# A hybrid decoder trunk on one core: the first quarter's gates by one 64-column matmul per token, GpSimd making all low weights of that stage, scatter from panel 11

## The chip, the cores and the metric

The kernel runs on one core of a Trainium2 chip. The metric is the device time of one execution in microseconds. Times of the kernel before are those of three runs; the profile is of one further execution of the same program.

## The reference

Two layers, each a token mixer (a gated short convolution in layer 0, latent attention in layer 1) and then a PEER mixer, which is the part that matters here. 256 tokens of 1024 channels; 8 heads; 128 keys per half; 16384 experts, of which each token and head takes 16:

```python
q = (xc @ w_q).reshape(C, PEER_HEADS, 2, PEER_HALF)
s = jnp.einsum("chpd,hpnd->chpn", q, subkeys).astype(jnp.float32)
top_s, top_i = lax.top_k(s, PEER_TOPK)
cand = top_s[:, :, 0, :, None] + top_s[:, :, 1, None, :]
best_s, best_pos = lax.top_k(cand.reshape(C, PEER_HEADS, PEER_TOPK * PEER_TOPK), PEER_TOPK)
ia = jnp.take_along_axis(top_i[:, :, 0], best_pos // PEER_TOPK, axis=-1)
ib = jnp.take_along_axis(top_i[:, :, 1], best_pos % PEER_TOPK, axis=-1)
expert = ia * PEER_KEYS + ib
g = jax.nn.softmax(best_s, axis=-1).astype(xc.dtype)
act = jax.nn.gelu(jnp.einsum("chkd,cd->chk", u_tab[expert], xc), approximate=False) * g
return jnp.einsum("chk,chkd->cd", act, v_tab[expert])
```

## The kernel before, in words

The PEER mixer is not gathered. The kernel multiplies all tokens with all experts: 128 panels of `peer_u` (one first key each, 128 experts by 1024 channels), then the gelu, then a weight that is zero for experts not chosen, then 128 panels of `peer_v`. Float32 products are made of two reduced parts (float32r): ScalarE makes the high part of a panel (`split_hi`, a cast of `raw` to `w_hi`), and GpSimd or VectorE the low part (`split_lo`, `raw` minus `w_hi` to `w_lo`). A panel has 4 slots for raw and high parts, 2 for low ones. The low part of panel j waits for its high part and until panel j-2 is multiplied; the loading of panel j+4 waits for the low part of panel j. On TensorE a panel is 16 matmuls with the high part (L588, L589) and 8 with the low part (L593), each 256 columns.

Per layer the PEER mixer goes through these stages:

- *search* ("sel"): 22 panels, 16 of them queries. VectorE takes the best 16 of each half and of their sums (`select`, L1404 to L1448).
- *ahead*: 26 panels of `peer_u` (j = 0 to 25). In the first half VectorE ends `select`: it decodes ranks into rows and columns and key numbers (L1470 to L1526, the *decode*). `dec_done` tells TensorE that tile t is decoded, and TensorE turns it (`turn`, 33 matmuls) in front of panel `TURN[t]` = 11 or 13. ScalarE copies what was turned (`turned`), and VectorE splits the gates (`gate_part`).
- from panel `SCATTER` = 13 on, the gates of the first quarter of the first keys are *scattered*: 16 groups of 16 tokens, spread over the 13 panels by `groups_after`. For a group VectorE makes one-hot matrices of the second key (`second_key_hots`, L1538) and of the first key times the gate's two parts (`first_key_hots`, L1542 and L1547 twice). TensorE then does two matmuls of 32 columns per token, which sum the parts in the bank (`scatter`, L655). The two banks take turns by group, and ScalarE copies a bank out (`copy_gates`, L1007).
- *mix*: three loops over 64 panels, alternately `peer_u` and `peer_v`, which also scatter the next quarters' gates, and *last*, 32 panels of `peer_v`. There a group is one matmul of 64 columns per token (`scatter_side`, L643), which leaves the two parts side by side over both banks; ScalarE copies the first part (`copy_first`, L1015) and VectorE adds the second (`add_gates`, L1557).

The order on each engine is written out by hand. Low parts: GpSimd makes all of the convolution, the attention and the search and the first `POOL_AHEAD` = 6 of the ahead stage (`select_panels`). VectorE makes the other 20 of the ahead stage: eight inside the decode (`next_lo`), the rest one after each panel's groups (`experts`), and all of mix and last. GpSimd's queue otherwise holds loads of the modulation's rows (L1301), one per wait on VectorE.

After the last group VectorE multiplies the first weights (`weigh`), ScalarE and VectorE split them, and TensorE takes them in the first `peer_v` panel; meanwhile it clears four banks (L703) and does the first wide panel of mix (L609, L614).

Of the kernel before, what the change touches and what calls it, by code (L numbers as in the profile page):

```python
# [56 lines left out]
POOL_AHEAD = 6  # L57
EXP_AFTER = 5
TURN = (11, 13)
SCATTER = 13  # L60
# [49 lines left out]
def program(nc, xT_in, c_in, pos_in, vec_in, con_in, ada_in, pan_in, key_in, iota_in, u_in, v_in, out):  # L110
    ctx = ExitStack()
    with ctx:
# [334 lines left out]
        def _(pe):  # L447
# [199 lines left out]
            def scatter(l, par, count):  # L647

                pe.wait_ge(hot_ready, count)
                pe.wait_ge(g_read, count)  # L650
                hb = hot_b[:, par, :].rearrange("p (t b) -> p t b", t=GT)
                hg = hot_g[:, par, :].rearrange("p (t x a) -> p t x a", x=2, t=GT)
                for t in range(GT):
                    for x in range(2):
                        mm = pe.matmul(GB[par][:, t * QUART:(t + 1) * QUART], hb[:, t, :], hg[:, t, x, :],  # L655
                                       start=(x == 0), stop=(x == 1))
                mm.then_inc(g_done, 1)

            def peer(l):
# [34 lines left out]
                for j in range(AHEAD - EARLY):  # L694
# [3 lines left out]
                    for g in groups_after(j) if j >= SCATTER else ():  # L698
                        if g == 1:
                            pe.wait_ge(idx_copied, TT * (l + 1))  # L700
                        scatter(l, g % 2, 64 * l + g + 1)
# [236 lines left out]
        def _(act):  # L938
# [65 lines left out]
            def copy_gates(quarter, par, count, token0):  # L1004
                act.wait_ge(g_done, count + 2)
                g = arena[:, quarter % 2 * QUART * T:(quarter % 2 + 1) * QUART * T].rearrange("p (a t) -> p a t", t=T)
                nc.scalar.copy(g[:, :, bass.ds(token0, GT)], GB[par][:].rearrange("p (t a) -> p a t", a=QUART)  # L1007
                               ).then_inc(g_read, 1)

# [13 lines left out]
            def peer(l):  # L1023
# [27 lines left out]
                for j in range(AHEAD - EARLY):  # L1051
# [14 lines left out]
                    for g in groups_after(j) if j >= SCATTER else ():  # L1066
                        copy_gates(0, g % 2, 64 * l + g + 1, g * GT)
# [200 lines left out]
        def _(pool):  # L1268
# [11 lines left out]
            def select_panels(l):  # L1280
                for j in range(len(SEARCH)):
                    split_lo(f"sel{l}", j)
                for j in range(POOL_AHEAD):
# [11 lines left out]
            for j in range(KB):  # L1295
                split_lo("conv_out", j)
            select_panels(0)
            with pool.Fori(0, 96 - ADA_FIRST) as it:
                pool.wait_ge(ada1_used, it + 1)
                pool.sem_inc(ada_seen, 1)  # L1300
                pool.dma_start(ada1[:], ada_in[bass.ds(it + ADA_FIRST, 1)].rearrange("o p n -> p (o n)")  # L1301
                               ).then_inc(ada1_landed, 16)
# [729 lines left out]
```

## Time and profile before

| what | us |
| --- | --- |
| median of three runs | 1899.36 |
| lowest, highest | 1897.52, 1900.22 |
| the profiled execution's own time | 1898.04 |
| its span, first to last instruction | 1896.4 |
| TensorE busy | 1879.8 |
| VectorE busy | 1579.3 |
| ScalarE busy | 1023.6 |
| GpSimd busy | 308.3 |

Busy times are sums over the span, and TensorE's ends are modelled, so that a busy TensorE may still be one that is short of something. The ahead stage of layer 0 lies between 205 and 299 us, that of layer 1 between 1150 and 1244.

### The profile page before, as it was taken

The numbers are of one execution on the slowest core, as the hardware profiler recorded it, in microseconds if no ns is written. First come the engines' busy times: TensorE is split into PE (matmuls) and PEld (weight loads), VectorE is DVE, ScalarE is ACT, GpSimd is POOL, SyncE is SP. The second block draws the span as 40 slices with busy tenths as digits, with TensorE's granted clock in tenths as the row PEclk, the third lists the DMA queues.
The fourth block names the chain that finished last, engine by engine and source line by source line (L and its number), as shares of the span: only waits on it lengthen the run. The fifth ranks groups of instructions, "written<-read, shape, count | busy, mean of one in ns | idle before, by whom it ended". The sixth has DMA issues, their size and how long they took to land.

```text
span 1896.4 us, 39962 instructions
## 1 busy us (share of the span) xinstructions
PE 1879.8 (99%) x13150; PEld 1667.1 (88%) x13150; DVE 1579.3 (83%) x3083; ACT 1023.6 (54%) x1658; POOL 308.3 (16%) x177
## 2 busy tenths in 40 slices
PE   9999999999999999999999999999999999999999
PEld 8999998888888888887889999988888888888887
DVE  6758999999999999997765489988888888888866
ACT  4354555555555555554455545555555555555553
POOL 3877500000000000000063574000000000000000
PEclk8999999999999999999999999999999999999999
DMA  9965646777777767777732355456556556556564
GB/s 360 365 209 163 199 133 188 225 229 226 220 228 226 231 224 227 224 229 228 230 107 89 129 161 168 134 169 182 182 177 182 183 179 183 181 179 185 178 191 141
DMA packets 104153, 371.77 MB, mean 196 GB/s; under 512 B 11393, under 2 KB 13825, under 8 KB 103681
## 3 DMA queue, kind: packets, MB, share of 16 engines
q1 hardware_dynamic: 96000, 341.26, 56.7%
q0 software_dynamic: 8064, 29.36, 5.1%
q8 instruction: 52, 0.85, 0.2%
q14 instruction: 37, 0.30, 0.1%
HBM read 369.53 MB, written 1.05 MB: 195 GB/s over the span
## 4 chain that ended last, share of the span: by engine, by line
PE 90%; DVE 5%; ACT 1%; DMA 1%; DVEq 1%; issue 1%; POOL 1%; SPq 0%; ACTq 0%; POOLq 0%
PE bank L624 36%; PE bank L609 17%; PE bank L614 9%; PE bank L588 5%; PE bank L593 5%; PE bank L589 5%; PE bank L643 2%; PE bank L655 1%; DVE w_lo L1321 1%; POOL w_lo L1277 1%; PE bank L671 1%; PE bank L885 1%; DVE arena L1407 1%; PE bank L453 1%; DVE arena L1448 1%
## 5 line engine op out<-in xcount | busy, mean ns | idle before, releaser
L944 ACT CAST w_hi<-raw 128x1024 fp32r<-128x1024 f32 (+1 forms) x603 | 631.2, 1047 | 324.1 <-DMA raw<-in_v_panels 129.4
L1321 DVE TENSOR_TENSOR w_lo<-raw,w_hi 128x1024 fp32r<-128x1024 f32 x488 | 596.8, 1223 | 119.4 <-PE bank L624 52.3
L609 PE MATMUL bank<-act_two,w_hi 128*128 128x512 f32 x1536 | 379.3, 389 | 0.0
L609 PEld LDWEIGHTS bank<-act_two,w_hi 128*128 128x128 f32 x1536 | 288.3, 188 | 59.8
L624 PE MATMUL bank<-w_hi,wt_hi 128*128 128x512 f32 x1024 | 328.0, 401 | 1.4 <-DVE wt_lo L1583 0.8
L624 PE MATMUL bank<-w_lo,wt_hi 128*128 128x512 f32 x1024 | 318.1, 391 | 0.0
L624 PE MATMUL bank<-w_hi,wt_lo 128*128 128x512 f32 x1024 | 317.1, 390 | 0.0
L1277 POOL TENSOR_TENSOR w_lo<-raw,w_hi 128x1024 fp32r<-128x1024 f32 (+2 forms) x115 | 273.6, 2382 | 150.2 <-PE bank L593 54.8
L588 PE MATMUL bank<-act_two,w_hi 128*128 128x256 f32 x984 | 246.1, 288 | 0.0
L589 PE MATMUL bank<-act_two,w_hi 128*128 128x256 f32 x984 | 241.2, 283 | 0.0
L624 PEld LDWEIGHTS bank<-w_hi,wt_lo 128*128 128x128 f32 x1024 | 192.3, 188 | 42.1
L624 PEld LDWEIGHTS bank<-w_lo,wt_hi 128*128 128x128 f32 x1024 | 192.2, 188 | 41.7
L614 PEld LDWEIGHTS bank<-act_two,w_lo 128*128 128x128 f32 x1536 | 209.5, 190 | 15.0
L614 PE MATMUL bank<-act_two,w_lo 128*128 128x256 f32 x1536 | 213.8, 282 | 0.0
L997 ACT COPY ring_g<-bank 128x256 f32 (+1 forms) x192 | 71.7, 374 | 253.9 <-PE bank L614 253.8
L624 PEld LDWEIGHTS bank<-w_hi,wt_hi 128*128 128x128 f32 x1024 | 177.8, 189 | 31.3 <-DVE w_lo L1321 3.6
L589 PEld LDWEIGHTS bank<-act_two,w_hi 128*128 128x128 f32 x984 | 188.5, 192 | 0.0
L588 PEld LDWEIGHTS bank<-act_two,w_hi 128*128 128x128 f32 x984 | 188.2, 191 | 0.0
L1538 DVE TENSOR_TENSOR hot_b<-ib_t,iota 128x2048 bf16<-128x2048 bf16 x128 | 156.0, 1219 | 0.3 <-PE bank L655 0.2
L1301 POOL DMA_DIRECT2D ada<-in_ada_rows x56 | 29.9, 534 | 688.1 <-DVE ada_sum L1347 688.1
L593 PE MATMUL bank<-act_two,w_lo 128*128 128x256 f32 x984 | 138.5, 283 | 0.0
L593 PEld LDWEIGHTS bank<-act_two,w_lo 128*128 128x128 f32 x984 | 127.2, 192 | 0.0
(249 smaller groups left out, 2057.5 us busy)
## 6 DMA issues: line engine op xcount, KB each, us to landing
raw<-in_u_panels SPq DMA_DIRECT2D x256, 512.0 KB, 3.7
raw<-in_v_panels SPq DMA_DIRECT2D x256, 512.0 KB, 3.7
raw<-in_panels SPq DMA_DIRECT2D x81, 512.0 KB, 4.0
ada<-in_ada_rows POOLq DMA_DIRECT2D x56, 512.0 KB, 4.8
arena<-in_ada_rows SPq DMA_DIRECT2D x40, 512.0 KB, 6.6
raw<-in_panels SPq DMA_DIRECT2D x6, 384.0 KB, 3.1
arena<-in_subkeys SPq DMA_DIRECT2D x2, 1024.0 KB, 6.4
xT<-in_xT SPq DMA_DIRECT2D x1, 1024.0 KB, 7.1
```

The lines of the kernel that those rows point to most:

```text
L588: pe.matmul(bank, w_hi[:, hi_slot, w], acts[0][k], start=(k == 0), stop=False)
L589: pe.matmul(bank, w_hi[:, hi_slot, w], acts[1][k], start=False, stop=False)
L593: mm = pe.matmul(bank, w_lo[:, lo_slot, w], acts[0][k], start=False, stop=(k == KB - 1))
L609: pe.matmul(bank[:, 0:2 * T], w_hi[:, hi_slot, w], act_two[:, :, a], start=(k == 0), stop=False, skip_group_check=True)
L614: mm = pe.matmul(bank[:, 0:T], w_lo[:, lo_slot, w], act_hi[:, a], start=False, stop=(k == KB - 1), skip_group_check=True)
L624: mm = pe.matmul(YB[2 * t + n][:], wt[:, par, a], (w_hi, w_lo)[v][:, slots[v], n * 512:(n + 1) * 512], start=False, stop=False, skip_group ...
L643: mm = pe.matmul(GB[t // (GT // 2)][:, o:o + 2 * QUART], hb[:, t, :], hg[:, t, :], start=True, stop=True)
L944: nc.scalar.copy(w_hi[:, slot, 0:width], raw[:, slot, 0:width]).then_inc(hi_done, 1)
L997: nc.scalar.copy(ring_g[:, bass.ds(slot * T, T)], bank[:, T:2 * T]).then_inc(lo_copied, 1)
L1277: pool.tensor_tensor(w_lo[:, lo_slot, 0:width], raw[:, slot, 0:width], w_hi[:, slot, 0:width].bitcast(F32), ALU.subtract).then_inc(lo_done, 1)
L1321: dve.tensor_tensor(w_lo[:, lo_slot, 0:width], raw[:, slot, 0:width], w_hi[:, slot, 0:width].bitcast(F32), ALU.subtract).then_inc(lo_done, 1)
L1538: dve.tensor_tensor(wide(hot_b[:, par, :]), each(ib_t, KEYS, token0), numbers(0, KEYS), ALU.is_equal)
```

## The change

- The first quarter's groups use `scatter_side`, `copy_first` and `add_gates` like the later ones; `scatter` and `copy_gates` go. The addition of group g-1 stands behind the one-hots of group g on VectorE; that of the last group stands in front of `weigh`.
- GpSimd makes the low parts of all 26 ahead panels. VectorE makes none of them; its first one is that of mix's panel 0, now behind the last one-hots. Its wait on `lo_done` keeps the count in order.
- `TURN` is (9, 11) and `SCATTER` 11: the turns stand two panels earlier, and the 16 groups are spread over 15 panels: one after each of the panels 11 to 24, two after panel 25.
- GpSimd's first load of a modulation row goes in front of layer 0's search; the loop has one round less.

```diff
-POOL_AHEAD = 6
 EXP_AFTER = 5
-TURN = (11, 13)
-SCATTER = 13
+TURN = (9, 11)
+SCATTER = 11
...
                     for g in groups_after(j) if j >= SCATTER else ():
-                        if g == 1:
+                        if g == 0:
                             pe.wait_ge(idx_copied, TT * (l + 1))
-                        scatter(l, g % 2, 64 * l + g + 1)
+                        scatter_side(l, g % 2, 64 * l + g + 1)
...
                     for g in groups_after(j) if j >= SCATTER else ():
-                        copy_gates(0, g % 2, 64 * l + g + 1, g * GT)
+                        copy_first(0, 64 * l + g + 1, g * GT)
...
-                for j in range(POOL_AHEAD):
+                for j in range(AHEAD - EARLY):
                     split_lo(f"ahead{l}", j)
...
+            load_ada1(0)
             select_panels(0)
...
                         first_key_hots(0, g % 2, g * GT)
-                    split_lo(*((f"ahead{l}", j + 1) if j + 1 < AHEAD - EARLY else (f"mix{l}", 0)))
+                        if g:
+                            add_gates(0, 64 * l + g, (g - 1) * GT)
                     if j == SCATTER:
                         gate_part(l, 1)
+                dve.wait_ge(lo_done, ring(f"ahead{l}", AHEAD - EARLY - 1)[3] + RAW)
+                split_lo(f"mix{l}", 0)
+                add_gates(0, 64 * l + FIRST, (FIRST - 1) * GT)
                 weigh(0, 0, 64 * l + 16 + 2)
```

The eight calls of `next_lo` in `select` go as well. In the order of VectorE's instructions, the piece from the decode's last wide additions to the low part behind the first group of one-hots reads before, in layer 0 (`w_lo` is a low part, `hot_b`, `hot_a` and `hot_g` are one-hots):

```order
L1516 TENSOR_TENSOR arena<-arena,iota 128x4096
L1321 TENSOR_TENSOR w_lo<-raw,w_hi 128x1024
L1427 CAST arena<-g_t 128x128
L1429 TENSOR_TENSOR arena<-g_t,arena 128x128
L1524 TENSOR_TENSOR arena<-arena 128x4096
L1321 TENSOR_TENSOR w_lo<-raw,w_hi 128x1024
L1538 TENSOR_TENSOR hot_b<-ib_t,iota 128x2048
L1542 TENSOR_TENSOR hot_a<-ia_t,iota 128x512
L1547 TENSOR_TENSOR hot_g<-hot_a,gh_t 128x16x32
L1547 TENSOR_TENSOR hot_g<-hot_a,gl_t 128x16x32
L1321 TENSOR_TENSOR w_lo<-raw,w_hi 128x1024
```

In the changed kernel the same piece, up to the second group, has other line numbers:

```order
L1490 TENSOR_TENSOR arena<-arena,iota 128x4096
L1412 CAST arena<-g_t 128x128
L1414 TENSOR_TENSOR arena<-g_t,arena 128x128
L1497 TENSOR_TENSOR arena<-arena 128x4096
L1510 TENSOR_TENSOR hot_b<-ib_t,iota 128x2048
L1514 TENSOR_TENSOR hot_a<-ia_t,iota 128x512
L1519 TENSOR_TENSOR hot_g<-hot_a,gh_t 128x16x32
L1519 TENSOR_TENSOR hot_g<-hot_a,gl_t 128x16x32
L1412 CAST arena<-g_t 128x128
L1414 TENSOR_TENSOR arena<-g_t,arena 128x128
```

The low parts are gone from between the decode's instructions and the one-hots. A later group of the changed kernel reads so on VectorE, with the addition of the group before it at its end:

```order
L1510 TENSOR_TENSOR hot_b<-ib_t,iota 128x2048
L1514 TENSOR_TENSOR hot_a<-ia_t,iota 128x512
L1519 TENSOR_TENSOR hot_g<-hot_a,gh_t 128x16x32
L1519 TENSOR_TENSOR hot_g<-hot_a,gl_t 128x16x32
L1529 TENSOR_TENSOR arena<-bank,arena 128x32x8 x2
```

The addition's pair stands where a low part of a panel stood. GpSimd's queue before, over the convolution, search and ahead stages of layer 0 (24 + 8, 22 and 6 panels) and the loop of row loads:

```order
L1277 TENSOR_TENSOR w_lo<-raw,w_hi 128x1024 x60
L1298 UNCONDITIONAL_BRANCH
L1298 ISA
L1301 ISA
L1301 DMA ada<-in_ada_rows 128x1024
L1298 REGISTER_ALU
L1298 COMPARE_AND_BRANCH
```

and the same piece of the changed kernel:

```order
L1258 TENSOR_TENSOR w_lo<-raw,w_hi 128x1024 x32
L1281 DMA ada<-in_ada_rows 128x1024
L1258 TENSOR_TENSOR w_lo<-raw,w_hi 128x1024 x48
L1286 UNCONDITIONAL_BRANCH
L1286 ISA
L1281 ISA
L1281 DMA ada<-in_ada_rows 128x1024
L1286 REGISTER_ALU
L1286 COMPARE_AND_BRANCH
```

Sixty low parts in front of the loop have become eighty, with one load in their middle.

## Rows read from the trace of the kernel before

**Rows 1.** The page: span, then busy us, share and instructions of each engine

```profile
span 1896.4 us, 39962 instructions
PE 1879.8 (99%) x13150; PEld 1667.1 (88%) x13150; DVE 1579.3 (83%) x3083; ACT 1023.6 (54%) x1658; POOL 308.3 (16%) x177
```

**Rows 2.** Windows: stretch, its length, engines' busy us (PE, PEld, DVE, ACT, POOL), clock, DMA

```profile
219.50:246.20 26.70, 26.64 (x245) 26.40 (x245) 24.82 (x33) 17.75 (x29) 0.81 (x2) 1.00 0.56 181
246.20:299.00 52.80, 52.80 (x846) 52.24 (x845) 51.11 (x80) 28.52 (x48) 0.00 (x0) 1.00 0.43 131
...
1191.50:1244.00 52.50, 52.50 (x835) 51.94 (x834) 51.00 (x80) 28.09 (x47) 0.00 (x0) 1.00 0.43 132
```

**Rows 3.** Timeline of TensorE: start, length, engine, line, op, out<-in, shape, count

```profile
170.45 1.12 PE L593 MATMUL bank<-act_two,w_lo 128*128 128x256 f32 x8
...
173.33 1.12 PE L593 MATMUL bank<-act_two,w_lo 128*128 128x256 f32 x8
...
237.29 2.21 PE L689 MATMUL bank<-ident_b,arena 128*128 128x128 bf16 x32
...
256.83 1.12 PE L593 MATMUL bank<-act_two,w_lo 128*128 128x256 f32 x8
257.79 0.96 PE L655 MATMUL bank<-hot_g,hot_b 128*128 128x32 f16 x32
...
260.61 1.12 PE L593 MATMUL bank<-act_two,w_lo 128*128 128x256 f32 x8
...
308.47 0.64 PE L643 MATMUL bank<-hot_g,hot_b 128*128 128x64 f16 x16
```

**Rows 4.** ScalarE's copy, VectorE's addition (ns min/median/max); TensorE's timeline after the stage

```profile
L1015 ACT COPY arena<-bank x192: 372/376/382, 309.2 to 1799.6; 128x256 f32 x168, 128x256 f32<-128x256 f32 x24
...
L1557 DVE TENSOR_TENSOR arena<-bank,arena x192: 412/415/418, 311.2 to 1800.7; 128x256 f32 x168, 128x256 f32<-128x256 f32 x24
...
298.74 1.16 PE L703 MATMUL bank<-act_two,zero 128*128 128x512 f32 x4
```

**Rows 5.** Search stage: L1448's durations; timelines of VectorE and GpSimd at 205 us

```profile
L1448 DVE TENSOR_TENSOR arena<-arena x64: 159/191/2422, 148.3 to 1162.8; 128x32 f32<-128x32 f32 x32, 128x48 f32<-128x48 f32 x16, 128x16 f32<-128x16 f32 x16
...
205.23 2.71 DVE L1448 TENSOR_TENSOR arena<-arena 128x32 f32<-128x32 f32 x4
...
205.27 2.41 POOL L1277 TENSOR_TENSOR w_lo<-raw,w_hi 128x1024 fp32r<-128x1024 f32 x1 [1.38 <-PE bank L593]
```

**Rows 6.** Norm in front of the search: timelines of VectorE and GpSimd

```profile
134.42 3.25 DVE L1375 SCALAR_TENSOR_TENSOR act_two<-ring_g,mod,act_two 128x256 fp32r<-128x256 f32 x8
...
136.11 6.17 POOL L1277 TENSOR_TENSOR w_lo<-raw,w_hi 128x1024 fp32r<-128x1024 f32 x2 [5.76 <-PE bank L474]
```

**Rows 7.** End of the convolution: timelines of VectorE and GpSimd

```profile
125.96 0.42 DVE L1395 TENSOR_TENSOR arena<-bank,arena 128x256 f32<-128x256 f32 x1 [0.49 <-ACT arena L988]
...
125.10 2.40 POOL L1277 TENSOR_TENSOR w_lo<-raw,w_hi 128x1024 fp32r<-128x1024 f32 x1 [0.48 <-PE bank L593]
```

**Rows 8.** Timeline of VectorE in the scatter stage: low part, one-hots, next one-hots

```profile
259.37 1.22 DVE L1321 TENSOR_TENSOR w_lo<-raw,w_hi 128x1024 fp32r<-128x1024 f32 x1
260.50 1.22 DVE L1538 TENSOR_TENSOR hot_b<-ib_t,iota 128x2048 bf16<-128x2048 bf16 x1
...
262.81 1.22 DVE L1538 TENSOR_TENSOR hot_b<-ib_t,iota 128x2048 bf16<-128x2048 bf16 x1
```

**Rows 9.** Timeline of VectorE in the decode

```profile
225.38 0.42 DVE L1493 SCALAR_TENSOR_TENSOR arena<-arena 128x256 f32<-128x256 f32 x1
225.71 0.42 DVE L1494 SCALAR_TENSOR_TENSOR arena<-arena 128x256 f32<-128x256 f32 x1
...
234.92 2.29 DVE L1524 TENSOR_TENSOR arena<-arena 128x4096 bf16<-128x4096 bf16 x1
```

**Rows 10.** Between the layers: TensorE's timeline, then a window as in rows 2

```profile
951.20 3.76 PE L544 MATMUL bank<-con,arena 128*128 128x1 f32 x32 [0.24 <-ACT arena L958]
...
954.80:958.10 3.30, 3.30 (x12) 2.68 (x12) 1.36 (x5) 0.94 (x3) 0.00 (x0) 0.50 0.19 78
```

More of the change, by code:

```diff
@@ L645, in scatter_side @@
                 mm.then_inc(g_done, 1)
[L647 to L657, printed above, removed]
             def peer(l):
@@ L1002, in gelu_sum @@
                 nc.scalar.activation(g, g, ACT.Gelu).then_inc(u_gelu, 1)
[L1004 to L1008, printed above, removed]
             def copy_first(quarter, count, token0):
@@ L1296, in _, with load_ada1 @@
                 split_lo("conv_out", j)
-            select_panels(0)
[L1298 to L1302, printed above, removed]
+            def load_ada1(n):
+                pool.wait_ge(ada1_used, n + 1)
+                pool.sem_inc(ada_seen, 1)
+                pool.dma_start(ada1[:], ada_in[bass.ds(n + ADA_FIRST, 1)].rearrange("o p n -> p (o n)")
+                               ).then_inc(ada1_landed, 16)
+            load_ada1(0)
+            select_panels(0)
+            with pool.Fori(1, 96 - ADA_FIRST) as it:
+                load_ada1(it)
             pool.wait_ge(lo_done, ring("last0", 31)[3] + RAW)
@@ L1463, in select @@
                 bv = hk(best_v)
-                lows = iter(range(POOL_AHEAD, SCATTER + 1))
-                def next_lo():
-                    split_lo(f"ahead{l}", next(lows))
                 dve.tensor_tensor(hk(gate), bv, bv[:, :, 0:1].broadcast_to([P, TT * HEADS, TOPK]), ALU.subtract
@@ L1482, in select @@
                 dve.drain()
-                dve.wait_ge(lo_done, ring(f"ahead{l}", POOL_AHEAD - 1)[3] + RAW)
-                next_lo()
                 dve.scalar_tensor_tensor(out=row_f, in0=dec_u[:, 1, :], scalar=-6.0, in1=row_f, op0=ALU.add, op1=ALU.max)
@@ L1491, in select @@
                 dve.drain()
-                next_lo()
                 dve.scalar_tensor_tensor(out=col_f, in0=row_f, scalar=16.0, in1=col_f, op0=ALU.mult, op1=ALU.min)
@@ L1499, in select @@
                 dve.drain()
-                next_lo()
                 for x, f in enumerate((row_f, col_f)):
@@ L1506, in select @@
                 dve.reciprocal(esum, esum)
-                next_lo()
                 dve.drain()
@@ L1517, in select @@
                     dve.drain()
-                    next_lo()
                     if t == 0:
@@ L1527, in select @@
                     dve.sem_inc(dec_done, 1)
-                    next_lo()
             each = lambda a, n, token0: (a[:, bass.ds(token0 * DUP, GT * DUP)].rearrange("p (t r) -> p t r", r=DUP)
@@ L1640, in mix_body @@
                         sum_products(it * 4 + (96 * l + 32 * q + 2 * s + 2), PAN[1], it * 4 + (2 * s + 1))
-                        add_gates(q + 1, it * 2 + (48 * l + 16 * q + s + 1), token0)
+                        add_gates(q + 1, it * 2 + (64 * l + 16 * (q + 1) + s + 1), token0)
                         if end and s:
```

## The prediction, made before the changed kernel had run

> **What bounds the kernel now.** I read the page first [rows 1]: TensorE (PE) is busy for 99% of the span, and the chain that ended last is its own work, so anything that TensorE no longer does is time gained, and anything it has to wait for is time lost. Then I read the two stretches that the change touches, layer 0's decode (219.5 to 246.2 us) and its scatter (246.2 to 299), and layer 1's scatter [rows 2]. The reader should see three things. TensorE is full in all of them: 26.64 of 26.70 us and 52.80 of 52.80. VectorE (DVE) is nearly full too, 24.82 and 51.11. GpSimd (POOL) does nothing, 0.81 and 0.00. The change relieves TensorE a little and moves work from the nearly full VectorE to the idle GpSimd. So the question is whether GpSimd and VectorE can work at the same time, and I looked for places in the trace where they already do.
>
> **What the change takes from TensorE.** A panel alone repeats every 2.88 us (170.45 to 173.33), one with a scatter group every 3.78 (256.83 to 260.61) [rows 3]. The group's 32 matmuls of 32 columns are a row of 0.96 us. The same work as 16 matmuls of 64 columns is already done in the later quarters, in a row of 0.64. That is 0.32 us less per group, 16 groups per layer: **-5.1 us per layer**, and TensorE alone would then need 3.46 us per panel and group. Moving the turns (one is a row of 2.21 us [rows 3]) from panels 11 and 13 to 9 and 11, and spreading the groups over 15 panels instead of 13, adds or removes no matmul.
>
> **What it adds behind the groups.** The first quarter now uses both banks for each group, so scatter g waits until ScalarE has copied the first parts of group g-1 and VectorE has added the second. Such a copy is two instructions of 0.376 us, such an addition two of 0.415 [rows 4], some 0.8 per group each. Inside the stage this hides in the 2.88 us of the next panel. It does not hide in the last panel, which has two groups in a row: copy and addition stand between them, about 1.6 us. After the last group one addition joins the chain to the first weights, which has over 4 us of panel and clearing work as cover (that begins at 298.74 [rows 4]); I take 0.3. Together +1.9 per layer. Were this all, the sum would be -5.1 + 1.9 = -3.2 per layer.
>
> **What moves from VectorE to GpSimd.** Before, GpSimd makes the low weights of panels 0 to 5 and is done with them as the decode begins [rows 2]; VectorE makes the other 20. After, GpSimd makes all 26. One takes 2.4 us on GpSimd (205.27 to 207.68 [rows 5]). That fits TensorE's pitch of 2.88 or 3.46 if nothing disturbs it. One low weight goes out of every VectorE round, 1.13 us (259.37 to 260.50 [rows 8]), and 0.8 of addition comes in.
>
> **Do they disturb each other?** Yes, in this trace. VectorE's additions of L1448 have both inputs in SBUF. They last 159 ns at least and 191 in the median, but up to 2422 [rows 5]. The case at 205.23 shows why: a group of four such additions lasts 2.71 us in all, while GpSimd's low weight holds 205.27 to 207.68. VectorE's second addition ended only with it. In the other direction, GpSimd became ready at 136.11 while a run of eight two-input instructions of VectorE went on from 134.42 to 137.67; its two splits last 6.17 us in place of twice 2.40 [rows 6]. It got in when the run was over, and then held VectorE's way for its full length. An addition with one input in PSUM is not touched: at 125.96 one took 0.42 us in the middle of a GpSimd split of 2.40 [rows 7]. So two-input VectorE work and GpSimd splits exclude each other, first come first served; I price one split at 2.3 us of exclusion ((6.17 - 1.56) / 2, what the two took once that run was over). The new additions of gates read a bank and are free.
>
> On this the Trainium skill speaks against the change: "SBUF — State Buffer", section "Who interferes with whom", says that a VectorE instruction with two SBUF inputs and a GpSimd instruction that reads SBUF contend for one read interface, and that the second fully blocks. The trace agrees for float32 [rows 5, 6]; no row here shows the bf16 forms beside GpSimd. By that rule the sum is the one that follows, without it the -3.2 above.
>
> **The sum of what must not overlap**, per layer, from 219.5 (the decode begins) to the last one-hots:
> - GpSimd: panels 6 to 25, 20 x 2.3 = 46.0 us.
> - Decode: eight additions of 256 elements that start 0.33 apart (225.38, 225.71), 2.6 us; four wide ones of 2.29 as the one at 234.92 (two of L1516, two of L1524), 9.2; two of 128 elements, some 0.2 each, 0.4 [rows 9]. 12.2 us.
> - One-hots: 260.50 to 262.81 is one group, four two-input instructions, 2.31 us [rows 8]. 16 x 2.31 = 37.0 us.
>
> 46.0 + 12.2 + 37.0 = 95.2 us, so the last one-hots are ready at 314.8 at the earliest, and the stage ends near 315.3 (half a microsecond for the last group's matmuls). It now ends at 298.74 [rows 4]. That is a floor of **+16.6 per layer**, with TensorE's gain already used up. In the scatter stage it reads as a round of 2.3 + 2.31 = 4.6 us against 3.46 for TensorE and 3.78 before.
>
> Above the floor lies time in which neither can use the way. The turn of tile 0 now comes at panel 9. TensorE reaches it at 237.29 - 2 x 2.88 = 231.5. Without exclusion VectorE would be ready at 231.5 as well: before, its last wide addition for tile 0 ended at 234.92 + 2.29 = 237.2 [rows 9], with five low weights of 1.13 in front of it. With it, four or five splits fall into this stretch. VectorE can use at most 3.5 us of them for one-input work. So TensorE waits 6 to 11 us at turn 0, in order, and with it the panels that free GpSimd's next slot. Most of this wait is in the floor already, since the splits and additions are counted there; what is new is only the time in which neither of them runs. I take 6 us for such holes: VectorE's drains and single-input instructions, the waits for turns and their copies (some 4), and a clock that may have fallen meanwhile. In the trace the granted clock fell to half after 3.7 us of one-column sums [rows 10]. A panel at half clock would take 5.76 instead of 2.88, and the row at half clock there is 3.3 us long, so a fall costs about 1.7.
>
> **+16.6 + 6 = about +23 per layer, +46 for both** (layer 1's scatter is 52.50 of 52.50 us on TensorE, the same picture [rows 2]). The profiled execution's own time is 1898.04 (span 1896.4); 1898.0 + 46 = 1944.0. The median of the three times is 1899.36, that is 1.3 above, so I forecast 1945. The bounds of the likeliest case: a floor with little on it, +17.5 per layer, 1934; holes of 15 us, for instance a phase in which GpSimd cuts in between the first and the last two one-hot instructions of each round and leaves 0.6 unused, +31, 1962.
>
> **Rivals.**
> - *Nothing in these stages is excluded* (the other side, **0.07**). For it: every blocked row is a float32 one of the search or the norm. Then VectorE's round is 2.31 + 0.8 = 3.1 and GpSimd's 2.40, both under 3.46; the place is the scatter stage, and it is decided by whether the round stays below TensorE's 3.46. -3.2 x 2 = -6.4 on the median of 1899.4: 1893.
> - *Only the float32 instructions are excluded* (**0.09**). The scatter stage then gains, and the decode's eight short additions meet four splits: 0 to 9 us at turn 0, less 3.2. Between -6 and +13 for both layers, 1893 to 1912, likeliest 1902.
> - *The clock falls again and again* (**0.08**). In the rounds of 4.6 us TensorE would be idle for 1.2, a quarter. For it: the fall at 954.8 came with the engine occupied, only thinly used [rows 10]. Against it: a round would still be three quarters dense panels, which ran at the full clock everywhere in rows 2, though there TensorE never waited. A panel and group at half clock would take 2 x 3.46 = 6.9 us instead of 4.6, for 15 panels up to +34 per layer beyond the forecast's +23: 1960, if a fifth of the stage is hit, to 2013.
> - *The change does not do what it says*: 64-column matmuls might cost here what 32-column ones do. The later quarters' row of 0.64 speaks against it, and under exclusion it would change nothing.
>
> **Chances.** The likeliest case has 0.76, the rivals 0.07, 0.09 and 0.08. A measurement of this kernel tells about 0.2%, 3.8 us, from no change. Faster by more: 0.07 + 0.03 of the second rival = 0.10. Within: 0.03. Slower: 0.87. The range 1926 to 1968 holds the likeliest case and the lower part of the clock rival, leaving out the two cases near or below 1912 (0.16) and the worst of the clock.
>
> **What would show it.** In the changed kernel's trace: one-hot instructions (hot_b, hot_a) or GpSimd splits of 3 to 4.5 us in place of 1.22, 0.42 and 2.40; scatter groups 4.6 us apart instead of 3.78; TensorE idle for 6 to 11 us before the first turn, waiting for VectorE; the gate additions still 0.41 each; a scatter row of 0.64; the quarters behind it unchanged. Wrong would be: no one-hot instruction over 1.3 us beside GpSimd (first rival), long decode additions but a round of 3.5 (second), or a granted clock of half inside the scatter stage (third).

## The result

The changed kernel takes 1951.82 us (median of four runs, 1948.16 to 1955.71), against 1899.65 for the kernel before. The ratio is 1.0277, 95% interval 1.0249 to 1.0305, so it is 52 us slower. The forecast was 1945 with a range of 1926 to 1968. The profiled execution took 1948.40, that is 50.4 more than the profiled one of before.

The page of the changed kernel (span; busy us, share and instructions of each engine; the chain that ended last, by engine), to be read against [rows 1]:

```profile
span 1946.7 us, 38966 instructions
PE 1878.1 (96%) x12638; PEld 1662.7 (85%) x12638; DVE 1628.6 (84%) x3107; ACT 1022.6 (53%) x1690; POOL 405.7 (21%) x217
PE 81%; DVE 13%; DVEq 2%; DMA 1%; ACT 1%; issue 1%; POOL 1%; SPq 0%; ACTq 0%; POOLq 0%
```

VectorE lost 40 low parts of 1.22 us and gained 64 additions (two per group) of 0.415, which is 22 us less work by the durations of before [rows 4, 8]. Yet it is busy for 49 us more. Its share of the chain that ended last is 13%, where it was 5%. The waits of TensorE say where it is waited for:

```profile
PE bank L642 <- DVE arena L1529: 30.1, 26, 3.6
PE bank L676 <- DVEq L1499: 20.5, 2, 10.5
PE bank L623 <- DVE w_lo L1306: 2.1, 2, 1.0
```

The columns are the waiting line, what it waited for, and us in total, times, longest. 30.1 us are waits in front of scatter groups, 20.5 us the two waits in front of a turn of tile 0. The third is new and small: mix's first low part on VectorE now stands behind the last one-hots.

TensorE and GpSimd at these places in layer 0, first TensorE at the turn of tile 0 and in two rounds of the scatter stage, then VectorE and GpSimd in the decode (start, length, engine, line, op, out<-in, shape, count, idle before and releaser):

```profile
242.36 3.63 PE L676 MATMUL bank<-ident_b,arena 128*128 128x128 bf16 x32 [10.54 <-DVEq L1499]
...
286.43 0.63 PE L642 MATMUL bank<-hot_g,hot_b 128*128 128x64 f16 x16 [1.21 <-DVE arena L1529]
...
290.92 0.63 PE L642 MATMUL bank<-hot_g,hot_b 128*128 128x64 f16 x16 [0.91 <-DVE arena L1529]
...
324.79 1.17 PE L690 MATMUL bank<-act_two,zero 128*128 128x512 f32 x4
```

```profile
220.72 2.35 DVE L1457 TENSOR_SCALAR arena<-arena 128x256 uint32<-128x256 uint32 x1
222.98 0.28 DVE L1458 TENSOR_SCALAR arena<-arena 128x256 uint32<-128x256 uint32 x1
...
226.47 2.46 DVE L1464 SCALAR_TENSOR_TENSOR arena<-arena 128x256 f32<-128x256 uint32 x1
...
229.22 2.50 DVE L1467 TENSOR_SCALAR arena<-arena 128x256 f32<-128x256 f32 x1
```

```profile
220.45 2.46 POOL L1258 TENSOR_TENSOR w_lo<-raw,w_hi 128x1024 fp32r<-128x1024 f32 x1 [0.48 <-PE bank L592]
...
231.97 2.45 POOL L1258 TENSOR_TENSOR w_lo<-raw,w_hi 128x1024 fp32r<-128x1024 f32 x1 [0.40 <-PE bank L592]
250.14 2.87 POOL L1258 TENSOR_TENSOR w_lo<-raw,w_hi 128x1024 fp32r<-128x1024 f32 x1 [15.73 <-PE bank L592]
```

In the decode every split of GpSimd lengthens one instruction of VectorE from 0.3 or 0.4 to about 2.5 us, once per panel. L1457 and L1458 are the same kind of instruction in the same shape; the first meets a split (220.45 to 222.91) and takes 2.35, the second doesn't and takes 0.28. So tile 0 is ready late, TensorE stands still for 10.5 us in front of its turn, and GpSimd, whose next slot is freed by TensorE, stands still for 15.73.

The scatter stage, VectorE over one group and the start of the next, and GpSimd beside it:

```profile
290.69 2.92 DVE L1510 TENSOR_TENSOR hot_b<-ib_t,iota 128x2048 bf16<-128x2048 bf16 x1
293.54 0.41 DVE L1514 TENSOR_TENSOR hot_a<-ia_t,iota 128x512 bf16<-128x512 bf16 x1
294.02 0.43 DVE L1519 TENSOR_TENSOR hot_g<-hot_a,gh_t 128x512 f16<-128x512 bf16 x1
294.36 0.42 DVE L1519 TENSOR_TENSOR hot_g<-hot_a,gl_t 128x512 f16<-128x512 bf16 x1
294.70 0.75 DVE L1529 TENSOR_TENSOR arena<-bank,arena 128x256 f32<-128x256 f32 x2
295.36 2.73 DVE L1510 TENSOR_TENSOR hot_b<-ib_t,iota 128x2048 bf16<-128x2048 bf16 x1
```

```profile
290.16 2.37 POOL L1258 TENSOR_TENSOR w_lo<-raw,w_hi 128x1024 fp32r<-128x1024 f32 x1 [2.30 <-PE bank L592]
294.65 2.36 POOL L1258 TENSOR_TENSOR w_lo<-raw,w_hi 128x1024 fp32r<-128x1024 f32 x1 [2.12 <-PE bank L592]
```

The split of 290.16 ends at 292.53, and the one-hot that had begun at 290.69 ends at 293.61, 1.1 us later: nearly its own length of 1.22 [rows 8]. It did nearly all of its work after the split. In the second pair the split begins with the addition, which reads a bank, is not touched (0.75 for two), and covers 0.7 us of the split. Rounds alternate between 4.49 and 4.68 us; before they were 3.78.

The stretches that answer to the first two of [rows 2] (length; busy us of PE, PEld, DVE, ACT, POOL; clock, DMA share, GB/s):

```profile
219.50:250.00 30.50, 19.96 (x162) 19.76 (x161) 27.26 (x29) 13.54 (x22) 12.70 (x6) 0.78 0.33 110
250.00:322.00 72.00, 58.90 (x648) 56.78 (x648) 69.84 (x91) 32.48 (x65) 36.69 (x15) 0.98 0.37 111
```

TensorE was full in both stretches before. The mark at which the first weights' stage begins, the clearing of the banks, stands at 324.79, against 298.74 [rows 4]: +26.1 us. In layer 1 it stands at 1293.84 against 1244.38 (the second row below, from the kernel before), +49.4, of which 23.3 came between the two marks, nearly all in layer 1's own stage. The remaining 0.9 of 50.4 came behind.

```profile
1293.84 0.94 PE L690 MATMUL bank<-act_two,zero 128*128 128x512 f32 x3
```

```profile
1244.38 1.16 PE L703 MATMUL bank<-act_two,zero 128*128 128x512 f32 x4
```

### The profile page after: what moved, and what is told of

It reads as the page before. It is cut to its first block, busy times and chain, and to the rows that moved or that the text cites. A ratio compares the mean times of both kernels' runs of the same rounds, so it can differ in the third digit from the quotient of the medians.

```text
span 1946.7 us, 38966 instructions
## 1 busy us (share of the span) xinstructions
PE 1878.1 (96%) x12638; PEld 1662.7 (85%) x12638; DVE 1628.6 (84%) x3107; ACT 1022.6 (53%) x1690; POOL 405.7 (21%) x217
## 4 chain that ended last, share of the span: by engine, by line
PE 81%; DVE 13%; DVEq 2%; DMA 1%; ACT 1%; issue 1%; POOL 1%; SPq 0%; ACTq 0%; POOLq 0%
PE bank L623 36%; PE bank L608 18%; PE bank L613 9%; DVE hot_b L1510 3%; PE bank L587 3%; PE bank L588 3%; PE bank L592 3%; PE bank L642 3%; DVE hot_g L1519 1%; DVE arena L1529 1%; DVE arena L1433 1%; DVEq L1516 1%; DMA raw<-in_panels 1%; DVE arena L1405 1%; DVE arena L1392 1%
## 5 line engine op out<-in xcount | busy, mean ns | idle before, releaser
L1306 DVE TENSOR_TENSOR w_lo<-raw,w_hi 128x1024 fp32r<-128x1024 f32 x448 | 548.0, 1223 | 117.4 <-PE bank L623 51.7
L1258 POOL TENSOR_TENSOR w_lo<-raw,w_hi 128x1024 fp32r<-128x1024 f32 (+2 forms) x155 | 371.0, 2397 | 241.2 <-PE bank L592 143.9
L623 PE MATMUL bank<-w_hi,wt_hi 128*128 128x512 f32 x1024 | 327.5, 400 | 3.2 <-DVE w_lo L1306 2.1
L623 PE MATMUL bank<-w_lo,wt_hi 128*128 128x512 f32 x1024 | 318.0, 391 | 0.0
L623 PE MATMUL bank<-w_hi,wt_lo 128*128 128x512 f32 x1024 | 317.2, 390 | 0.0
L623 PEld LDWEIGHTS bank<-w_hi,wt_lo 128*128 128x128 f32 x1024 | 192.3, 188 | 42.0
L623 PEld LDWEIGHTS bank<-w_lo,wt_hi 128*128 128x128 f32 x1024 | 192.2, 188 | 41.6
L623 PEld LDWEIGHTS bank<-w_hi,wt_hi 128*128 128x128 f32 x1024 | 178.0, 189 | 32.6 <-DVE w_lo L1306 4.6
L1510 DVE TENSOR_TENSOR hot_b<-ib_t,iota 128x2048 bf16<-128x2048 bf16 x128 | 191.0, 1492 | 0.4 <-issue 0.4
```

What stands on the lines that cost most here:

```text
L623: mm = pe.matmul(YB[2 * t + n][:], wt[:, par, a], (w_hi, w_lo)[v][:, slots[v], n * 512:(n + 1) * 512], start=False, stop=False, skip_group ...
L1258: pool.tensor_tensor(w_lo[:, lo_slot, 0:width], raw[:, slot, 0:width], w_hi[:, slot, 0:width].bitcast(F32), ALU.subtract).then_inc(lo_done, 1)
L1306: dve.tensor_tensor(w_lo[:, lo_slot, 0:width], raw[:, slot, 0:width], w_hi[:, slot, 0:width].bitcast(F32), ALU.subtract).then_inc(lo_done, 1)
L1510: dve.tensor_tensor(wide(hot_b[:, par, :]), each(ib_t, KEYS, token0), numbers(0, KEYS), ALU.is_equal)
```

## The experiments

The theory: two-input instructions of VectorE on SBUF, the bf16 one-hots too, and GpSimd's splits exclude each other. The rivals: it is TensorE's fallen clock, or the waits that the one-matmul form brings, or the early turns. All ratios are against the kernel before on the same chip. Ratios near 1 are given with their intervals.

**Half of GpSimd's work.** GpSimd's low parts of the ahead stage are made over 512 of 1024 columns, so half of those low parts is missing from the products:

```diff
                 width = D if unroll else WIDTHS.get(BASE[stage] + j, D)
+                if stage.startswith("ahead"):
+                    width = D // 2
```

> The changed kernel, but GpSimd's low parts of the ahead stage are 512 columns wide instead of 1024; the other half of these low parts is left out, TensorE's work and every wait stay. Theory (GpSimd's splits and VectorE's two-input instructions exclude each other): the price of a split falls from 2.3 to about 1.15 us, a round from 4.6 to 3.46 us, which is TensorE's own; the loss is gone but for some us: 1892 to 1908 us. Rival (the order is to blame: turns at 9 and 11 come too early for VectorE, both banks for one group chain copy and addition): nothing changes, 1948 to 1956.

Measured 1916.16 us, ratio 1.0070 (1.0044 to 1.0096): 39 of the 52 us are gone, 13 stay. VectorE and GpSimd in one round of it:

```profile
266.20 2.31 DVE L1512 TENSOR_TENSOR hot_b<-ib_t,iota 128x2048 bf16<-128x2048 bf16 x1
...
269.61 0.74 DVE L1531 TENSOR_TENSOR arena<-bank,arena 128x256 f32<-128x256 f32 x2
270.27 2.23 DVE L1512 TENSOR_TENSOR hot_b<-ib_t,iota 128x2048 bf16<-128x2048 bf16 x1
```

```profile
266.16 1.27 POOL L1260 TENSOR_TENSOR w_lo<-raw,w_hi 128x512 fp32r<-128x512 f32 x1 [2.79 <-PE bank L592]
270.16 1.27 POOL L1260 TENSOR_TENSOR w_lo<-raw,w_hi 128x512 fp32r<-128x512 f32 x1 [2.72 <-PE bank L592]
```

The split is half as long, and it now lengthens VectorE's round by 1.1 us. In the changed kernel that was 1.6 (a round of 4.58 less 2.31 of one-hots and 0.67 of additions): of the 2.3 that a split keeps the way, 0.7 lay under the additions. Neither the clock nor the new waits would do this to a one-hot. The measured time is above the 1892 to 1908 that I expected: I had taken the addition as cover for the split. But the split begins as the addition ends, so all of it falls on the one-hot. The round is 2.31 + 0.67 + 1.1, about the 4.0 that VectorE's rows show, and not TensorE's 3.46.

**GpSimd's low parts alone**, on the kernel before, with the old matmuls, turns and groups:

```diff
-POOL_AHEAD = 6
+POOL_AHEAD = AHEAD - EARLY
...
-                    split_lo(f"ahead{l}", next(lows))
+                    return
...
-                    split_lo(*((f"ahead{l}", j + 1) if j + 1 < AHEAD - EARLY else (f"mix{l}", 0)))
                     if j == SCATTER:
                         gate_part(l, 1)
+                dve.wait_ge(lo_done, ring(f"ahead{l}", AHEAD - EARLY - 1)[3] + RAW)
+                split_lo(f"mix{l}", 0)
```

> The kernel before with one thing of the change: GpSimd makes all 26 low parts of the ahead stage. Two matmuls of 32 columns per token, ScalarE's single copy, turns at 11 and 13 and scatter from 13 stay. Theory (exclusion): the sum of what must not overlap is the same 95 us per layer, so the same floor of +17 and a few us of holes: 1936 to 1948 us, with a round of 4.6 us per group. Rival (order and banks): faster or equal, 1893 to 1903, since VectorE is relieved and nothing else changed.

Measured 1946.71, ratio 1.0235 (1.0203 to 1.0266), as expected; four rounds in a row from 265.44 us on are 4.5 long. Its waits of TensorE have the same two places, with no addition in it, and its one-hots lengthen up to 3.41 us:

```profile
PE bank L655 <- DVE hot_g L1546: 17.7, 12, 3.5
PE bank L689 <- DVEq L1525: 16.5, 2, 8.9
```

```profile
L1537 DVE TENSOR_TENSOR hot_b<-ib_t,iota x128: 1210/1218/3409, 253.7 to 1839.1; 128x2048 bf16<-128x2048 bf16 x128
```

This part of the change alone loses 44 us, with the turns where they were before. What the rest of the change adds to it is not separated: 8 us by the ratios, whose intervals overlap, and 3 between the two profiled executions (1948.40 and 1945.37).

**The one-matmul form alone**, on the kernel before, VectorE keeping its low parts:

```diff
-                        if g == 1:
+                        if g == 0:
                             pe.wait_ge(idx_copied, TT * (l + 1))
-                        scatter(l, g % 2, 64 * l + g + 1)
+                        scatter_side(l, g % 2, 64 * l + g + 1)
...
-                        copy_gates(0, g % 2, 64 * l + g + 1, g * GT)
+                        copy_first(0, 64 * l + g + 1, g * GT)
...
-                    split_lo(*((f"ahead{l}", j + 1) if j + 1 < AHEAD - EARLY else (f"mix{l}", 0)))
+                        if j >= SCATTER and g == groups_after(j)[-1]:
+                            split_lo(*((f"ahead{l}", j + 1) if j + 1 < AHEAD - EARLY else (f"mix{l}", 0)))
+                        if g:
+                            add_gates(0, 64 * l + g, (g - 1) * GT)
```

> The kernel before with the other thing: one matmul of 64 columns per token, both banks per group, ScalarE copies the first part and VectorE adds the second (behind the next panel's low part); low parts, turns and scatter's start as before. Theory: no GpSimd beside the one-hots, so no blocked instruction. VectorE's round is 2.31 + 1.13 + 0.8 = 4.2 us against TensorE's 3.46, VectorE was full but for 1.7 us per layer and gets 16 x 0.8 = 12.8 more: +11 per layer, about 1921 us (1912 to 1928). Rival (the banks' chain makes the loss): 1940 or more, with TensorE waiting for the additions.

Measured 1923.38, ratio 1.0115 (1.0083 to 1.0147). The expectation was about 1921. No one-hot is longer than before, and yet it loses 20 us, for another reason. In its timeline of VectorE one round is

```profile
254.21 1.21 DVE L1538 TENSOR_TENSOR hot_b<-ib_t,iota 128x2048 bf16<-128x2048 bf16 x1
...
256.51 1.22 DVE L1321 TENSOR_TENSOR w_lo<-raw,w_hi 128x1024 fp32r<-128x1024 f32 x1
257.65 0.75 DVE L1557 TENSOR_TENSOR arena<-bank,arena 128x256 f32<-128x256 f32 x2
258.31 1.21 DVE L1538 TENSOR_TENSOR hot_b<-ib_t,iota 128x2048 bf16<-128x2048 bf16 x1
```

2.31 + 1.13 + 0.67 = 4.1 us, above TensorE's 3.46 and above the old 3.78. The additions don't fit beside the low parts, so the two halves of the change belong together: the first needs VectorE to be relieved, and the second relieves it in a way that costs more.

**The clock at the turn.** The changed kernel with 42 matmuls on zeros in front of the turn of tile 0, which fill the wait:

```diff
                 for j in range(AHEAD - EARLY):
+                    if j == TURN[0]:
+                        busy(GB[0], 42)
                     if j in TURN:
                         turn(TURN.index(j))
```

> The changed kernel with 42 matmuls on zeros (some 10 us) in front of turn 0, in the time in which TensorE waits for the decode. It tells what the fallen clock costs. If the clock matters as thought, it stays at 1.0 through the wait, turn 0 takes 2.1 us instead of 3.3 and panels 9 and 10 their 2.88: 2 to 4 us less per layer, 1941 to 1947. If it does not: 1948 to 1956 as the changed kernel. More than 1956 would say that the fill is longer than the wait.

> The fill in front of turn 0 again, now beside the changed kernel. If the fallen clock at the turns costs its share, it is 2 to 6 us below e7_change_again; if the time is set by GpSimd and VectorE alone, the two agree within 1.5 us.

```profile
231.79 9.71 PE L568 MATMUL bank<-zero 128*128 128x512 f32 x42
242.55 2.21 PE L676 MATMUL bank<-ident_b,arena 128*128 128x128 bf16 x32 [1.06 <-DVEq L1501]
```

The turn takes 2.21 us in place of 3.63, and the granted clock stays full around it. In the changed kernel it had fallen to half from 234.5 to 248.2:

```profile
234.50:248.20 13.70, 5.84 (x44) 5.85 (x45) 11.18 (x14) 3.10 (x7) 0.00 (x0) 0.50 0.12 38
```

(columns as in the windows above). 5.84 us of work at half clock would be 2.9 at the full one. But the turn begins no earlier (242.55 against 242.36), and most of what is gained behind it is given back in the scatter stage, whose rounds are the same 4.49 and 4.68: the end of the stage in layer 0 is 324.1, and 323.1 in the second run, against 324.8. At the end of layer 1's stage nothing is left of it (1293.64 and 1294.02, against 1293.84). Measured 1948.94 (1.0248, 1.0221 to 1.0275) on the chip of the three runs above, where 1941 to 1947 was expected if the clock mattered as thought, and 1949.23 (1.0257, 1.0238 to 1.0276) on a second chip, where the changed kernel took 1952.64 (below). That is 3.4 us less by the medians, with ratio intervals that overlap, so the size is known only to some us. But 46 us of loss on the first chip and 48 on the second stay although the clock at the turn is full: the fallen clock there is not the cause.

**The changed kernel once more**, on the chip of the second filled run; no edit.

> The changed kernel unaltered, beside the others on one chip, as their base: 1948 to 1956 us, ratio 1.025 to 1.030.

1952.64, ratio 1.0284 (1.0259 to 1.0310): the loss is the same on this second chip.

**The old decode.** VectorE again makes the low parts of panels 6 to 13 inside the decode, turns at 11 and 13, groups from panel 13. GpSimd makes the low parts from panel 14, and the groups stay one matmul:

```diff
+POOL_AHEAD = 6
-TURN = (9, 11)
-SCATTER = 11
+TURN = (11, 13)
+SCATTER = 13
...
-                for j in range(AHEAD - EARLY):
+                for j in range(POOL_AHEAD):
+                    split_lo(f"ahead{l}", j)
+                pool.wait_ge(lo_done, ring(f"ahead{l}", SCATTER)[3] + RAW)
+                for j in range(SCATTER + 1, AHEAD - EARLY):
                     split_lo(f"ahead{l}", j)
```

> The decode as before (VectorE makes the low parts of panels 6 to 13, turns at 11 and 13), the scatter stage as in the change (one matmul of 64 columns, GpSimd makes the low parts from panel 14 on), but from panel 13. It splits the loss into its two places. Exclusion in the scatter stage alone: 12 splits x 2.3 + 16 x 2.31 one-hots = 64.6 us against 51.7 for TensorE before (less 5 for the shorter matmuls), that is +12 to +15 per layer, 1924 to 1930 if the kernel before is at 1899.5 (ratio 1.013 to 1.016), no wait for the decode. If the decode were the place of the loss: ratio 0.997 to 1.003.

Measured 1941.08, ratio 1.0214 (1.0191 to 1.0237): well above what I expected, +20.0 us at the end of layer 0's stage (318.72 against 298.74) where I had +12 to +15. The turn of tile 0 is back at 237.3 without a wait, so the 20 us of waits there are gone. In the scatter stage TensorE now waits 36.0 us in both layers, where it was 30.1. Its timeline of VectorE in one group shows how:

```profile
266.13 3.41 DVE L1545 TENSOR_TENSOR hot_b<-ib_t,iota 128x2048 bf16<-128x2048 bf16 x1
269.46 0.41 DVE L1549 TENSOR_TENSOR hot_a<-ia_t,iota 128x512 bf16<-128x512 bf16 x1
269.95 0.43 DVE L1554 TENSOR_TENSOR hot_g<-hot_a,gh_t 128x512 f16<-128x512 bf16 x1
270.30 2.56 DVE L1554 TENSOR_TENSOR hot_g<-hot_a,gl_t 128x512 f16<-128x512 bf16 x1
```

Two splits (266.07 and 270.08 in GpSimd's timeline) hit one group, which took 7.3 us in place of 4.6. From 256 to 284 us the clock was at 0.76 in the mean:

```profile
256.00:284.00 28.00, 20.46 (x200) 19.92 (x201) 24.84 (x37) 10.99 (x25) 10.71 (x5) 0.76 0.25 78
```

So the early turns were not the cause: without them, and with eight low parts fewer per layer on GpSimd, most of the loss is still there.

**One operand in PSUM.** If the exclusion hangs on VectorE reading two operands from SBUF, an instruction that takes one of them from PSUM should go free. On the old-decode kernel, the key numbers that the big one-hot is compared with are copied into an unused part of bank 5, two bf16 numbers per float32 word, and read from there:

```diff
+            iota_p = ps[5][:, 0:KEYS // 2]
+            numbers_p = (iota_p.bitcast(BF16).rearrange("p (b r) -> p b r", r=DUP)
+                         .unsqueeze(1).broadcast_to([P, GT, KEYS // DUP, DUP]))
...
+                dve.tensor_copy(iota_p, iota[:].bitcast(F32))
+                dve.drain()
...
-                        second_key_hots(g % 2, 64 * l + g + 1, g * GT)
+                        second_key_hots_p(g % 2, 64 * l + g + 1, g * GT)
```

> As e6_old_decode of this call, and the key numbers that hot_b is compared with lie in a PSUM bank that is free at that time, so the second-key one-hots have one input in SBUF instead of two. Nothing else changes: same lengths, same order, GpSimd beside them. Exclusion of two-input instructions predicts that no hot_b is lengthened by a split any more, while hot_a and hot_g still are (to 2.5 us and more). If hot_b keeps its 1.22 us from PSUM, GpSimd's split can lie over it and over the gate additions, a round is about 2.3 + 1.17 = 3.5 us and the kernel is near or below the one before, ratio 0.995 to 1.003. If PSUM halves its rate (2.2 us), a round is about 4 us: ratio 1.004 to 1.010. If hot_b is lengthened as in the changed kernel, the two-input reading is wrong.

Measured 1927.28, ratio 1.0140 (1.0118 to 1.0161), 14 us below the kernel it is made from. Its rows show the mechanism (L1564 is the one-hot that reads the bank, L1549 the small one that doesn't; ns min/median/max):

```profile
L1564 DVE TENSOR_TENSOR hot_b<-ib_t,bank x32: 1204/1211/1222, 246.5 to 1269.0; 128x2048 bf16<-128x2048 bf16 x32
```

```profile
L1549 DVE TENSOR_TENSOR hot_a<-ia_t,iota x128: 412/417/2118, 247.6 to 1824.8; 128x512 bf16<-128x512 bf16 x128
```

```profile
277.76 1.21 DVE L1564 TENSOR_TENSOR hot_b<-ib_t,bank 128x2048 bf16<-128x2048 bf16 x1
...
279.72 2.64 DVE L1554 TENSOR_TENSOR hot_g<-hot_a,gl_t 128x512 f16<-128x512 bf16 x1
```

32 of 32 big one-hots take their undisturbed 1.21 us beside GpSimd's splits (the one of 277.76 beside a split of 276.04 to 278.55), where the same one-hots had taken up to 3.41. The split now catches the next instruction that has both operands in SBUF. That is why I missed the size: a round still loses up to a whole split, as long as any such instruction is left in it.

**All operands of the stage.** The small one-hot reads its numbers, and the gate products their gate parts, from PSUM too; ScalarE copies the repeated gate parts there:

```diff
+                    i.then_inc(spread_here, 1)
+                    act.wait_ge(spread_here, TT * l + t + 1)
+                    for x, to in enumerate((gh_t, gl_t)):
+                        i = nc.scalar.copy(ps[2 + t][:, x * T:(x + 1) * T], to[:].bitcast(F32)[:, t * T:(t + 1) * T])
...
-                        first_key_hots(0, g % 2, g * GT)
+                        first_key_hots_p(g % 2, g * GT)
```

> As e5_psum_numbers, and the other three one-hot instructions of the first quarter also have one input in PSUM (the key numbers for hot_a, the repeated gate parts for both hot_g, copied there by ScalarE). GpSimd's splits lie beside them from panel 14 on. If only instructions with two inputs in SBUF are excluded, nothing in the scatter stage is lengthened, VectorE's round is its own 2.98 us, and TensorE (3.43 per panel and group) sets the pace but for the second group of three panels, which waits some 2 us for the shared banks: 13 x 2.88 + 16 x 0.55 + 3 x 2 = 52.2 us against 51.7 before, ratio 0.998 to 1.003. If blocking stays, 1.008 and more.

Measured 1903.57 (12 runs), ratio 1.0012 (1.0001 to 1.0023), within what was expected.

```profile
L1570 DVE TENSOR_TENSOR hot_b<-ib_t,bank x32: 1209/1211/1223, 247.6 to 1246.3; 128x2048 bf16<-128x2048 bf16 x32
```

```profile
L1581 DVE TENSOR_TENSOR hot_g<-hot_a,bank x64: 412/418/425, 249.2 to 1248.2; 128x512 f16<-128x512 bf16 x64
```

Nothing is lengthened. GpSimd makes the low parts from panel 14 on, VectorE adds all gates, and a round is 3.43 us, TensorE's own. 37 us against the old-decode kernel are gone (1.0012 against 1.0214, on two chips), by moving operands and adding the small copies that put them there. It still doesn't beat the kernel before. TensorE's timeline where a panel has two groups tells why:

```profile
265.37 0.64 PE L645 MATMUL bank<-hot_g,hot_b 128*128 128x64 f16 x16
267.63 0.63 PE L645 MATMUL bank<-hot_g,hot_b 128*128 128x64 f16 x16 [1.62 <-DVE arena L1591]
```

16 groups on 13 panels make three such pairs per layer, and copy and addition stand between the two groups of each: 3 x 1.62 = 4.9 us, nearly the 5.1 that the matmuls save. From the turn of tile 1 to the clearing of the banks it is 53.8 us in both layers (246.23 to 300.01, 1196.55 to 1250.37) against 53.5 before (245.21 to 298.74, 1190.85 to 1244.38), so the stage costs 0.3 us per layer more. The rest of what this profiled execution took beyond that of before, 7.0 us in all, lies in stretches that the change does not touch. It was 1.0 us late already at 129 us, in front of the search, and 4.6 came between the stage of layer 0 and 1081 us, where the granted clock was 0.74 from 1000 to 1020 us and 1.00 in the same stretch before.

**Groups between the halves of a panel.** On that kernel, twelve groups go between a panel's high and low products, four stay behind panels 13, 17, 21 and 25, so that panel work stands between most groups:

```diff
+ENDS = {13: (0,), 17: (5,), 21: (10,), 25: (15,)}
+MIDS = {14: 1, 15: 2, 16: 3, 17: 4, 18: 6, 19: 7, 20: 8, 21: 9, 22: 11, 23: 12, 24: 13, 25: 14}
...
+                if between is not None:
+                    between()
                 pe.wait_ge(lo_done, n + RAW)
```

> As e8_all_from_psum, but the 16 groups are not two at the end of a panel: twelve of them stand between the high and the low part of panels 14 to 25, four behind panels 13, 17, 21 and 25, some 3 us apart. No group waits 2 us for the banks any more; VectorE's 16 rounds of 2.98 us (47.7) and TensorE's 46.2 are level. Expected: the stage takes 47 to 49 us instead of 51.7, the chain behind it 0.5 to 1 more, so 2 to 4 us less per layer than before: ratio 0.9955 to 0.999. If VectorE's rounds turn out longer (bank reads slower than SBUF): ratio 1.000 to 1.005.

Measured 1901.98 (12 runs; the kernel before 1900.70 on this chip), ratio 1.0012 (1.0001 to 1.0023), a miss. The pairs that remain (one group in the middle of a panel, one at its end) are still 2.26 us apart, and the first addition waits 1.4 us for ScalarE. TensorE's waits in front of groups fell from 10.3 to 7.7 us:

```profile
PE bank L651 <- DVE arena L1601: 7.7, 12, 1.3
```

From the turn of tile 1 to the clearing of the banks it takes 53.2 and 52.9 us in the two layers, 0.3 and 0.6 less than before. That is too little to be seen in the whole time: no version that I found is faster than the kernel before.

## Why the prediction was right

- **TensorE's saving, -5.1 per layer: as said.** A group is a row of 0.63, and where nothing is excluded the rounds came to 3.43 against the 3.46 of the sum. In the changed kernel none of it reaches the end.
- **The end of the stage, +1.9:** the last two groups stand 2.5 apart with 1.88 of waiting, where I had 1.6. The last addition is covered as assumed. What I did not price is the low part of mix's first panel, which now comes 1.0 us per layer late (L623 <- L1306). Layer 0's lies in the 23.3 between the marks, layer 1's in the 0.9 behind them.
- **Exclusion, also of the bf16 forms: shown.** The step that the sum hung on was that a rule seen on float32 rows [rows 5, 6] holds for bf16 one-hots. hot_b goes up to 3.29 us beside a split; with splits of half the length its excess in a round is 1.1 us where it was 1.6; one operand in PSUM ends it. The additions that read a bank stay at 0.41 each, as at 125.96 [rows 7].
- **The floor, +16.6 per layer:** 20 splits fall between 219.5 and the end of the stage in layer 0 (the five from 220.45 to 231.97, fifteen from 250.14 on), each 2.36 to 2.66 us, except for one of 2.87 that starts inside a one-hot. A round of 4.6 was forecast; the rounds from 281 to 318 us are 4.49 and 4.68, mean 4.58.
- **The turn, 6 to 11 us of idle TensorE:** 10.5 in layer 0, 9.9 in layer 1.
- **The holes, the term that was mis-sized.** I took 6 us per layer in which neither side uses the way. Layer 1 had 23.3 - 16.6 = 6.7, layer 0 26.1 - 16.6 = 9.5. The largest one is inside GpSimd's idle 15.73 us in front of 250.14. From 234.4 to 249.5 VectorE's decode has only 10.7 us of two-input work in a stretch of 15.1 (three short ones of 0.42, four wide of 2.29, one of 0.29), so 4.4 us are empty. They are casts, a reduction and the wait of 1.86 for ScalarE's turned copy. Layer 0 has a second stop at 268 to 275. There two splits had hit one group (a round of 7.19), the clock fell for 3.4 us, and VectorE then waited 0.97 for ScalarE. The clock was at half for 13.7 us at the turn and not for one row as in my 1.7. By the filled wait this was worth some 3 us in both layers, a size that is not clear of the noise.
- Together: 26.1 + 23.3 + 0.9 = 50.4 (the parts are rounded) in the profiled execution against 46. The median lies 3.4 above that execution, where I had put 1.3. Of its four executions two took 1948 us with a mean granted clock of 0.988, and two 1955 with 0.984 and 0.985; none of the second kind was profiled, so where their 7 us lie is open.
- In the second rival my upper end does not follow: (9 - 3.2) x 2 is 11.6 and not 13, so 1911. It changes no chance.

One detail of the mechanism was off: I thought that single-input work could run beside a split, and allowed 3.5 us for it that rest on no row. In the decode the float32 and uint32 TENSOR_SCALARs with one SBUF operand are held up as well (2.35, 2.50). The Trainium skill, "SBUF — State Buffer", section "Who interferes with whom", says so too, of single-source tensor_scalar and copies in a 2-port mode. I take it that this cost little, since the split would have met the next instruction anyway; no run shows it.

Of the rivals, *nothing is excluded* and *only the float32 instructions are excluded* fell with the first row of hot_b above 1.3 us. They were not far-fetched: with all operands of the stage in PSUM the exclusion ends there, and the time is 1903.57 (though without the change's early turns). *The clock falls again and again* did not come true in the changed kernel (0.98 in the scatter stretch), but it did in the old-decode kernel, 0.76 over 28 us, where rounds went up to 7.3. *The change does not do what it says* fell with the row of 0.63.

## What to carry to other kernels

Before work is moved from a full VectorE to an idle GpSimd, look for a row in which the two already meet, and add up the splits and all VectorE instructions with SBUF operands as if they ran on one engine; here 95 us of such work per layer stood in 80 us. If the move is wanted all the same, bring one operand of each VectorE instruction to PSUM: that removed the loss where halving the splits, moving the turns back or filling the wait didn't. It was tried only with the eight low parts of the decode left on VectorE. And a form that saves TensorE time but puts an addition between two groups gains only where panel work stands between all groups.

## What the runs showed of the hardware

- A bf16 one-hot of 128x2048 that reads one operand from a PSUM bank (bf16 pairs written there as float32 words) takes 1211 ns in the median, against 1218 with both operands in SBUF; reading the bank costs nothing, and it frees the instruction from GpSimd's splits.
- A split of GpSimd holds VectorE's next fitting instruction for its whole length, whichever that is: a cheap 0.41 us hot_a or hot_g pays as much (2.63, 2.56) as the big one-hot. Taking one kind of instruction out of the way only moves the hit.
- In the changed kernel's stage of layer 0 GpSimd's splits hardly lengthen (2.36 to 2.87) while VectorE's instructions do. So GpSimd's row in the page looks healthy, and the loss is booked as VectorE's busy time. The reverse happens too: a split that became ready inside a long instruction of VectorE took 3.31 us in the old-decode kernel (246.43, beside a hot_b of 246.26) and 4.21 with GpSimd's low parts alone (240.12, beside a wide instruction of 239.85 to 242.13).
- TensorE's granted clock was at half from 234.5 to 248.2 us: TensorE had been out of work from 231.8 on, and worked again from 242.4 on. With 9.7 us of matmuls on zeros in the wait it stayed full.
- Not settled: why the old-decode kernel had groups hit by two splits over and over while the changed one settled into even rounds after 281 us. No run varied the phase of the two engines alone.
